# RWKV block of a two-part transformer: decay bias in the matrix product, other order of pieces, gate products moved to the end

## What is computed

```
r, k, v, w_lr, a_lr, g_lr = split(token_shift(p, mu))
log_decay = -softplus(-(w0 + tanh(w_lr) @ w2)) - 0.5
decay = exp(-exp(log_decay))           # = exp(-e^-0.5 * sigmoid(w0 + tanh(w_lr) @ w2))
a = sigmoid(a0 + a_lr @ a2)
g = sigmoid(g_lr) @ g2
kk = heads(k * k_k);  kk = kk / max(sqrt(sum(kk * kk)), 1e-12)
...                                     # recurrence over tokens, 8 heads of 64
y = group_norm(y) * ln_w + ln_b
y = (y + bonus) * g
merged = g_ret * (y_ret @ p_ret) + g_dsa * (y_dsa @ p_dsa) + g_rwkv * (y @ p_rwkv)
```

## Time and profile before

| what | value |
|---|---|
| median of 3 runs | 2798.94 us (2798.51 to 2799.71) |
| profiled execution | 2798.51 us, its span 2796.7 us |
| TensorE products / weight loads busy | 2599.5 us (93%) / 2008.1 us (72%) |
| VectorE / ScalarE busy | 1274.0 us (46%) / 836.0 us (30%) |
| mean granted TensorE clock | 0.987 |
| chain that ended last | TensorE 69%, DMA 20%, VectorE 6%, ScalarE 2% |

### The profile page before, as it was taken

How to read it: one execution, slowest core, us unless ns; L and a number is a source line. 1 busy time by engine, 2 the same in 40 slices (tenths; PEclk the granted TensorE clock), 3 DMA queues, 4 the chain that set the end, 5 groups by cost and what they waited for, 6 DMA issues and landing times.

```text
span 2796.7 us, 46123 instructions
## 1 busy us (share of the span) xinstructions
PE 2599.5 (93%) x19503; PEld 2008.1 (72%) x19503; DVE 1274.0 (46%) x1875; ACT 836.0 (30%) x1051; POOL 0.2 (0%) x4
## 2 busy tenths in 40 slices
PE   8899888879899888879999999999999999999998
PEld 8743433348543333369999899999899898899998
DVE  4610101037411000055566765655655658766555
ACT  4300000025210000033343442443433444523433
POOL 0000000000000000000000000000000000000000
PEclk9999999999999999999999999999999999999999
DMA  8689999973899999955563441455555544323553
GB/s 270 264 357 425 426 425 425 426 286 106 329 400 425 425 425 425 426 192 181 181 230 122 135 140 59 137 166 181 181 181 181 192 152 150 107 77 107 166 181 136
DMA packets 286519, 685.17 MB, mean 245 GB/s; under 512 B 11992, under 2 KB 217616, under 8 KB 236944
## 3 DMA queue, kind: packets, MB, share of 16 engines
q1 hardware_dynamic: 282792, 671.27, 63.6%
q10 hardware_dynamic: 3560, 11.45, 1.1%
HBM read 681.63 MB, written 1.05 MB: 244 GB/s over the span
## 4 chain that ended last, share of the span: by engine, by line
PE 69%; DMA 20%; DVE 6%; ACT 2%; issue 1%; DVEq 1%; SPq 0%; ACTq 0%; POOLq 0%
PE psum L419 68%; DMA weight_ring<-in_w_gate 14%; DMA weight_ring<-in_w_up 3%; DMA weight_ring<-in_w_down 2%; DVE weight_ring_parts L2066 1%; PE psum L427 1%; ACT weight_ring_parts L2058 1%; DVEq L552 1%; DMA weight_ring<-in_w_in_a 0%; DVE arena L3260 0%; SPq L1921 0%; DMA h_tok<-in_mem 0%; DMA weight_ring<-in_w_in 0%; DVE arena L1837 0%; DVE small L2778 0%
## 5 line engine op out<-in xcount | busy, mean ns | idle before, releaser
L419 PE MATMUL psum<-weight_ring_parts,arena_parts 128*128 128x256 f32 (+1 forms) x2992 | 666.4, 315 | 6.3 <-DVE arena_parts L2159 1.9
L2066 DVE TENSOR_TENSOR weight_ring_parts<-weight_ring,weight_ring_parts 128x2048 fp32r<-128x2048 f32 x217 | 496.5, 2290 | 338.0 <-ACT weight_ring_parts L2058 332.0
L419 PE MATMUL psum<-x_chan_parts,weight_ring_parts 128*128 128x256 f32 x3200 | 612.2, 282 | 12.9 <-DVE arena_parts L2155 7.7
L2058 ACT ACTIVATE weight_ring_parts<-weight_ring 128x2048 fp32r<-128x2048 f32 x217 | 414.9, 1913 | 465.7 <-POOLq L532 345.4
L419 PE MATMUL psum<-weight_ring,arena 128*64 128x512 f32 (+1 forms) x2112 | 474.8, 582 | 73.8 <-DMA weight_ring<-in_w_gate 39.1
L419 PEld LDWEIGHTS psum<-weight_ring_parts,arena_parts 128*128 128x128 f32 x2992 | 496.4, 189 | 42.9 <-issue 3.3
L419 PEld LDWEIGHTS psum<-x_chan_parts,weight_ring_parts 128*128 128x128 f32 x3200 | 509.0, 190 | 18.3 <-issue 12.9
L419 PE MATMUL psum<-arena 64*64 64x64 f32 (+7 forms) x4616 | 467.0, 335 | 29.3 <-DVE arena L1837 15.6
L419 PEld LDWEIGHTS psum<-weight_ring,arena 128*64 128x64 f32 (+1 forms) x2112 | 179.3, 140 | 361.4 <-issue 358.5
L419 PE MATMUL psum<-weight_ring_parts,x_chan_parts 128*128 128x256 f32 x2336 | 427.5, 285 | 2.3 <-DVE arena_parts L2155 2.2
L419 PE MATMUL psum<-arena_parts,weight_ring_parts 128*128 128x256 f32 x1536 | 419.0, 283 | 0.0
(11 more groups left out here) (324 smaller groups left out, 1713.6 us busy)
## 6 DMA issues: line engine op xcount, KB each, us to landing
weight_ring<-in_w_gate SPq DMA_DIRECT2D x92, 1024.0 KB, 23.2
weight_ring<-in_w_up SPq DMA_DIRECT2D x92, 1024.0 KB, 22.9
weight_ring<-in_w_in SPq DMA_DIRECT2D x70, 1024.0 KB, 5.0
arena<-in_w_down SPq DMA_DIRECT2D x64, 1024.0 KB, 22.5
weight_ring<-in_w_down SPq DMA_DIRECT2D x64, 1024.0 KB, 23.2
weight_ring<-in_ffa_w_in SPq DMA_DIRECT2D x44, 1024.0 KB, 7.1
weight_ring<-in_ffb_w_in SPq DMA_DIRECT2D x44, 1024.0 KB, 5.7
arena<-in_w_gate SPq DMA_DIRECT2D x36, 1024.0 KB, 18.5
```

What stands on the lines that cost most here:

```text
L419: return nc.tensor.matmul(*args, **kw)
L2058: nc.scalar.activation(HIGH[buf], ring[:, sl, :], ACT.Copy).then_inc(s_hi, 1)
L2066: nc.vector.tensor_tensor(ring_parts[:, sl, :], ring[:, sl, :], f32(HIGH[buf]), ALU.subtract).then_inc(s_split, 1)
```

## The change

The bias becomes one row, which TensorE adds to the decay piece with a product of a row of ones by the bias row. ScalarE reads the decay pieces from PSUM. The two decay pieces come first, then the two of the rates. The sums are written in four pieces again, but first two of inclusive sums and then two of exclusive ones, each for 256 channels; the exponentials follow suit. VectorE's low part of load 34 stands ahead of its reading of the head sums. The gate groups 2, 1, 1, 2 behind the solve are taken out and the last 12 become 18. In the tail the gate g multiplies the finished sum once, where it multiplied its two terms beforehand.

```diff
-        W0B = sb("decay_bias_rows", [P, 512])
+        W0R = sb("decay_bias_row", [1, 512])
...
-            s.e.dma_start(W0B[:, :], a["rwkv_w0_2"][l].partition_broadcast(P)).then_inc(s_load["w0"], 16)
+            s.e.dma_start(W0R[0:1, :], a["rwkv_w0_2"][bass.ds(l, 1), :]).then_inc(s_load["w0"], 16)
...
+            pe.e.wait_ge(s_load["w0"], pe.c["l_w0"].next())
...
-                pe.mm(ps[:, b, :], LR[0:64, 0, t * P:(t + 1) * P], LORA[0:64, :], start=True, stop=True).then_inc(s_full[b], 1)
+                pe.mm(ps[:, b, :], LR[0:64, 0, t * P:(t + 1) * P], LORA[0:64, :], start=True, stop=False)
+                pe.mm(ps[:, b, :], ones2[0:1, :], W0R[0:1, :], start=False, stop=True).then_inc(s_full[b], 1)
+            for c in range(0, 4, 2):
                 b = pe.take()
                 pe.e.wait_ge(s_free[b], pe.emptied())
                 for j in range(2):
-                    c = 2 * t + j
-                    last = pe.mm(ps[:, b, j * SEQ:(j + 1) * SEQ], LORA[64:128, c * P:(c + 1) * P],
+                    last = pe.mm(ps[:, b, j * SEQ:(j + 1) * SEQ], LORA[64:128, (c + j) * P:(c + j + 1) * P],
                                  LR[64:128, 0, :], start=True, stop=True)
                 last.then_inc(s_full[b], 1)
...
-            pe.e.wait_ge(s_a2p, pe.c["a2p"].next(T))
-            for c in range(4):
-                b = pe.take()
-                pe.e.wait_ge(s_free[b], pe.emptied())
-                for t in range(T):
-                    last = pe.mm(ps[:, b, t * 2 * P:(t + 1) * 2 * P], LWT[:, t, c * P:(c + 1) * P], cumulate,
-                                 start=True, stop=True)
-                last.then_inc(s_full[b], 1)
+            pe.e.wait_ge(s_free[(pe.pieces.n - 6) % BANKS], pe.read_out(pe.pieces.n - 6))
+
+            pe.e.wait_ge(s_free[(pe.pieces.n - 5) % BANKS], pe.read_out(pe.pieces.n - 5))
+            for m in (1, 0):
+                for c in range(0, 4, 2):
+                    b = pe.take()
+                    pe.e.wait_ge(s_free[b], pe.emptied())
+                    for j in range(2):
+                        for t in range(T):
+                            last = pe.mm(ps[:, b, j * SEQ + t * P:j * SEQ + (t + 1) * P],
+                                         LWT[:, t, (c + j) * P:(c + j + 1) * P], cumulate[:, m * P:(m + 1) * P],
+                                         start=True, stop=True)
+                    last.then_inc(s_full[b], 1)
...
-            gate_products(2)
             settled(4)
...
             for n in range(2):
-                gate_products(1)
...
-            gate_products(2)
             settled(4)
...
-            gate_products(12)
+            gate_products(18)
...
             for t in range(T):
-                s.skip()
-
-                s.e.wait_ge(s_v2a, s.c["v2a"].next(2 if t == 0 else 1))
-                nc.scalar.activation(LWT[:, t, :], LWT[:, t, :], ACT.Sigmoid).then_inc(s_a2p, 1)
+                b = s.take()
+                s.e.wait_ge(s_full[b], s.filled())
+                nc.scalar.activation(LWT[:, t, :], ps[:, b, :], ACT.Sigmoid).then_inc(s_free[b], 1)
...
-            nc.scalar.activation(RSS[:, :, :], RSS[:, :, :], ACT.Sqrt).then_inc(s_a2v, 1)
...
-            for c in range(4):
-                b = s.take()
-                s.e.wait_ge(s_full[b], s.filled())
-                sums = ps[:, b, :].rearrange("p (t m n) -> p m t n", t=T, m=2)
-                nc.scalar.activation(by_token_tile(PI, c), sums[:, 1], ACT.Exp, scale=-DECAY)
-                nc.scalar.activation(by_token_tile(IPI, c), sums[:, 1], ACT.Exp, scale=DECAY)
-                nc.scalar.activation(by_token_tile(PEX, c), sums[:, 0], ACT.Exp, scale=-DECAY).then_inc(s_free[b], 1)
+            s_root(RSS[:, :, :])
+            for c in range(0, 4, 2):
+                b = s.take()
+                s.e.wait_ge(s_full[b], s.filled())
+                nc.scalar.activation(flat(PI[:, c:c + 2, :]), ps[:, b, :], ACT.Exp, scale=-DECAY)
+                nc.scalar.activation(flat(IPI[:, c:c + 2, :]), ps[:, b, :], ACT.Exp, scale=DECAY).then_inc(s_free[b], 1)
+            for c in range(0, 4, 2):
+                b = s.take()
+                s.e.wait_ge(s_full[b], s.filled())
+                nc.scalar.activation(flat(PEX[:, c:c + 2, :]), ps[:, b, :], ACT.Exp, scale=-DECAY).then_inc(s_free[b], 1)
...
             v_merge_sparse(0)
+            v_ahead(34)
             v_rates_of_tokens(1.0, 1e-24, ALU.mult, ALU.max)
-            v.e.wait_ge(s_load["w0"], v.c["l_w0"].next())
-            rates = v.pieces.n + 1
-            for t in range(T):
-                b = v.take()
-                v.e.wait_ge(s_full[b], v.filled())
-                nc.vector.tensor_tensor(LWT[:, t, :], ps[:, b, :], W0B[:, :], ALU.add).then_inc(s_free[b], 1)
-                v.sync()
-                nc.vector.nop().then_inc(s_v2a, 1)
-                v.skip()
-            v_ahead(34)
-            v.skip(6)
+            rates = v.pieces.n + 2
+            v.skip(10)
             v_reciprocal_of_rates()
-
-            for n in (rates, rates + 2):
+            for n in (rates, rates + 1):
...
-            nc.vector.tensor_tensor(BON[:, :, :], BON[:, :, :], WG[:, :, :], ALU.mult)
-            v.sync()
-            nc.vector.tensor_tensor(YO[:, :, :], YO[:, :, :], WG[:, :, :], ALU.mult)
...
             v.sync()
+            nc.vector.tensor_tensor(YO[:, :, :], YO[:, :, :], BON[:, :, :], ALU.add)
+            v.sync()
             for c in (0, 2):
-                nc.vector.tensor_tensor(YO[:, c:c + 2, :], YO[:, c:c + 2, :], BON[:, c:c + 2, :], ALU.add).then_inc(s_v2a, 1)
+                nc.vector.tensor_tensor(YO[:, c:c + 2, :], YO[:, c:c + 2, :], WG[:, c:c + 2, :], ALU.mult).then_inc(s_v2a, 1)
```

More of the change, by code:

```diff
@@ L3091, in s_rwkv @@
                 for j in range(2):
-                    c = 2 * t + j
-                    last = nc.scalar.activation(WA[:, c, :], ps[:, b, j * SEQ:(j + 1) * SEQ], ACT.Sigmoid,
-                                                bias=pv("rwkv_a0")[:, c:c + 1])
+                    last = nc.scalar.activation(WA[:, c + j, :], ps[:, b, j * SEQ:(j + 1) * SEQ], ACT.Sigmoid,
+                                                bias=pv("rwkv_a0")[:, c + j:c + j + 1])
                 last.then_inc(s_free[b], 1)
@@ L3099, in s_rwkv @@
                 nc.scalar.activation(flat(WG[:, c:c + 2, :]), ps[:, b, :], ACT.Copy).then_inc(s_free[b], 1)
-            nc.scalar.activation(RSS[:, :, :], RSS[:, :, :], ACT.Sqrt).then_inc(s_a2v, 1)
-            def by_token_tile(x, c):
-                return x[:, c, :].rearrange("p (t n) -> p t n", t=T)
-            for c in range(4):
+            s_root(RSS[:, :, :])
+            for c in range(0, 4, 2):
                 b = s.take()
                 s.e.wait_ge(s_full[b], s.filled())
-                sums = ps[:, b, :].rearrange("p (t m n) -> p m t n", t=T, m=2)
-                nc.scalar.activation(by_token_tile(PI, c), sums[:, 1], ACT.Exp, scale=-DECAY)
-                nc.scalar.activation(by_token_tile(IPI, c), sums[:, 1], ACT.Exp, scale=DECAY)
-                nc.scalar.activation(by_token_tile(PEX, c), sums[:, 0], ACT.Exp, scale=-DECAY).then_inc(s_free[b], 1)
+                nc.scalar.activation(flat(PI[:, c:c + 2, :]), ps[:, b, :], ACT.Exp, scale=-DECAY)
+                nc.scalar.activation(flat(IPI[:, c:c + 2, :]), ps[:, b, :], ACT.Exp, scale=DECAY).then_inc(s_free[b], 1)
+            for c in range(0, 4, 2):
+                b = s.take()
+                s.e.wait_ge(s_full[b], s.filled())
+                nc.scalar.activation(flat(PEX[:, c:c + 2, :]), ps[:, b, :], ACT.Exp, scale=-DECAY).then_inc(s_free[b], 1)
             s.skip(2)
```

## The result

The changed kernel takes 2826.48 us, the median of 8 runs (2817.81 to 2839.44). The kernel before, run beside it, takes 2802.27 us (8 runs, 2798.51 to 2804.51). The ratio is 1.0083, 95% interval 1.0061 to 1.0105: about 24 us slower, where 6.5 us were forecast, and outside the range. Over all 33 executions of the changed kernel the times form two groups: 15 lie between 2814.8 and 2821.6 us, with a mean granted clock of 0.981 to 0.985, and 18 between 2824.4 and 2839.4 us, with 0.973 to 0.979. The kernel before has 0.987. The profiled execution (2830.59 us) is of the upper group.

A forecast was written before the change was run, and what follows sets the result against it. TensorE, busy for 93% of the span, was taken as the bound, with ScalarE pacing the decay stage. Decay 4.8 plus gate groups 1.7 gave 6.5 us on 2798.5, 2805.0, and 0.4 for the median: 2805.4 us, range 2801.5 to 2809.

The forecast's parts named there:

- The sign: Whole kernel: slower, 2805.4 us or +0.23%; chances slower 0.61, same 0.34, faster 0.05.
- TensorE's clock falls: Rival, decay stage: idle gaps lower the clock during WA1 to G1, up to 2.7 us a layer; chance 0.12.
- WA1 waits for the bank of the head sums: Decay stage: second rates piece waits for VectorE's late read of its PSUM bank; +2.5 and +2.1 us by layer.
- the row of four products: Decay stage: both decay pieces and both bias products at 0.90 us each, 3.6 us, finished before the bank is free.
- The total of this part: Decay stage, both layers: 2.5 + 2.1 + 0.2 = 4.8 us slower.
- My first rival: Decay stage: the late bank does not decide; 32 records in a row, 7.2 us; total 2800.8 to 2804.2; chance 0.24.
- One row costs what 64 or 128 cost: Decay stage: the one-row bias product taken at the 64-row product's full price, 0.90 us.
- Sums and exponentials, +0.1: Decay stage: new sums covered, reshaped exponentials end the head spreading 0.1 us later a layer.
- The bias row's load: ScalarE's queue behind the first FFN: 2 KB instead of 256 KB, effect nothing.
- Gate groups, +0.86 a layer: Solve and tail: six moved groups save 1.28 us and cost 2.14 at the end, 1.7 in all.
- The tail's extra pass, covered: Tail: VectorE's extra 1.3 us pass hidden behind 18 gate groups; without the moved groups it would cost 0.9.
- 0.2% as what can't be told: Whole kernel: a difference under 0.2% (5.6 us) is about what measurement can't tell from none.

The follow-up runs named there:

- e2: The changed kernel with the bias added by a product of 128 equal rows instead of one row; 2824.61 us, ratio 1.0068.
- e3: The changed kernel with the 128-row bias product and the gate groups back in their places behind the solve; 2818.53 us, ratio 1.0062.
- e1: The changed kernel with the gate groups 2, 1, 1, 2 back behind the solve and 12 at the end; 2819.43 us, ratio 1.0065.
- e7: The kernel before with only the one-row bias products added, VectorE copying where it added; 2814.52 us, ratio 1.0049.
- e12: The changed kernel with gate groups back and pieces in the order decay, bias, rates, decay, bias, rates; 2816.02 us, ratio 1.0057.
- e14: As e12, with VectorE reading the head sums ahead of the low part of load 34, as before; 2809.55 us, ratio 1.0031.
- e15: As e14, with the tail's two products by the gate back as in the kernel before; 2816.66 us, ratio 1.0061.
- e20: The kernel before with only the one-row bias products and the six gate groups moved to the end; 2819.81 us, ratio 1.0066.
- e5: The changed kernel with gate groups back and without the bias products (w0 left out); 2812.27 us, ratio 1.0048.
- e11: As e5, with the pieces in the order of before: decay, rates, decay, rates; 2815.55 us, ratio 1.0053.
- e17: The kernel before with only the low part of load 34 ahead of VectorE's read of the head sums; 2814.00 us, ratio 1.0048.
- c1: The kernel before, unchanged, run as a control under its own label; 2803.50 us, ratio 1.0005.
- e4: The kernel before with only the six gate groups moved to the end; 2803.24 us, ratio 1.0009.
- e4b: A repeat of e4 for another profile; 2804.36 us, ratio 1.0014.
- e13: As e11, with VectorE reading the head sums ahead of the low part of load 34, as before; 2809.15 us, ratio 1.0024.
- e16: The kernel before with only the new form of the sums and exponentials; 2801.51 us, ratio 1.0003.

## Why the prediction was wrong

The sign was right, the size was not. By its steps:

- **"TensorE's clock falls", chance 0.12, at most 2.7 us a layer: this is the step that failed.** It was priced as an idle between two bursts, for 2.71 us of products. What the runs show in its place is a fall while TensorE is busy, 13.7 and 10.2 us long, at 0.40 to 0.47 of its length: 6.5 us by e2 and e3 in layer 0, and 68.2 - 64.1 = 4.1 in layer 1. Count the decay stages of all profiled executions. With the bias products the clock falls in 14 of 18 passes (after, e1, e2, e3, e7, e12, e14, e15, e20, two layers each). Without them but with TensorE waiting 2.4 to 3.5 us for the head sums' bank it falls in 6 of 6 (e5, e11, e17). With neither it falls in 0 of 12 (before, c1, e4, e4b, e13, e16), though these have idles of up to 1.5 us. That the bias products and the late read each bring it down is shown.

What in the stretch with the bias products does it isn't: those with one and with 128 rows both do, and 4 of 18 passes escape. The traces narrow it down. In 10 of the 14 passes the fall comes 0.71 to 0.96 us behind the start of D0, and the first bias product begins only 1.09 to 1.34 us behind it; all ten last 13.7 us. D0 itself is already slowed there: 1.32 us for its records in layer 0 of after, 1.12 at 2.4 GHz. So in these passes it can't be the running of the bias product. What differs up to then is that D0 runs alone. In every kernel without the bias product a record of WA0 starts 0.01 us behind D0, as in this row of the kernel before, beside D0 at 1646.92 in the earlier trace rows:

```profile
1646.93 0.70 PE L419 MATMUL psum<-arena,norm_gain_bias 64*128 64x256 f32 x2
```

With the bias product WA0 starts 2.1 us behind D0 at the earliest. That D0 alone is what brings the clock down is argued, not shown: no run keeps WA0 from D0 without adding a product. That leaves the cause open, and with it how often the falls come; the medians of e14 and e13 lie together, those of e7 and the kernel before don't.

- **The fall seen as an idle gap.** The prediction weighed the rival by gaps alone. In e5, e11 and e17 the gap is there (2.4 to 3.5 us). Of the 14 falls with bias products 13 have none (in after, 14.00 us busy of 14, and 3.00 of 3 before them). The one in layer 1 of e12, which has the late read too, has a wait of 0.63 us for the head sums' bank ahead of it. The Trainium skill ("TensorE: Matmul & The Clock Gate", "Why this matters for your kernels") asks to avoid idle gaps between bursts; the first kind agrees with it, for the second the measurement decides.
- **The second fall, in the chunks.** 38.3 and 38.4 us with it (after, e2), 29.6 without (e4, e20): 8.7 us, with 20.5 us at 1.2 GHz. It came where two things met, a fall in the decay stage of the same layer and moved gate groups: in 2 of 4 such passes (layer 0 of after and of e2; not in layer 1 of after, nor in layer 0 of e20). With moved groups and no fall ahead of them it came in 0 of 6 passes, and with a fall and the groups in place in 0 of 16. Four passes are too few to call the link shown. It would explain part of the distance between the two groups of times, which is about 14 us; this is argued, not shown. The two groups of e2 fit it, e20 doesn't decide it. It stays open.
- **"WA1 waits for the bank of the head sums": the mechanism is right, its place in this kernel wrong.** The wait is there, 3.50, 3.21 and 3.31 us, once the bias products are gone. With them TensorE is its own bound. The term that was mis-sized is the row of four products, D0, D1 and the two bias products: 0.90 us each forecast, 1.05 measured. The sum had TensorE ready for WA1 4.5 us behind D0 (1651.4) and the bank free at 5.4 (1652.3). In layer 0 of e3, at full clock, the four take 4.2 us before WA0 begins, and the read of the head sums ends at 4.89, before WA1's turn. The table load then starts 8.78 us behind D0 where it was 6.29: +2.5 in layer 0, just as forecast, for another reason than the one given; that is luck. In layer 1 (e2) it is 8.78 against 5.60, +3.2 where 2.1 were forecast. The total of this part at full clock was 2.7 and 3.4 us for 2.6 and 2.2 forecast. Before, D and WA lie in different halves of the rows and run side by side, D0, WA0, D1 and WA1 together in about 2 us; the two bias products cost TensorE that overlap as well as their own length. My first rival (32 records in a row, 7.2 us) described it, with 7.97 us measured, and priced it at 0.8 us too little. The Trainium skill (the same page, "Packing small matmuls") says that products in different groups of rows run at once; the 12 records of D and WA side by side agree.
- **One row costs what 64 or 128 cost**: confirmed, 1.05 us for each (1.12 us for the pair of records).
- **Sums and exponentials, +0.1**: confirmed. e16 gives 0; e13 goes from D0 to the head spreading in 10.34 us against 10.20. The bias row's load: nothing, 424.7 against 424.8 to the Tanh.
- **Gate groups, +0.86 a layer**: 1.8 us saved instead of 1.28 (e4b). 2.1 are given back up to the next Square, as forecast (2.14), so +0.3 there; by the last Square of the program 2.4, so +0.6. The waits are those forecast.
- **The tail's extra pass, covered**: right. From the square of y to the next Square e4 and after both take 51.1 or 51.2 us, with the old tail and with the new one. Without the moved groups it costs 0.9 us, as forecast (e1: 50.0 against 49.1).
- **Chance between executions.** The prediction took 0.2% as what can't be told. The unchanged kernel's own 11 times span 9 us, its times beside all the runs 2797.44 to 2810.23, and kernels with falls that come and go span 20 and more (e20 20.3, e2 25.5). A range built from one trace has to allow for that. Also unexplained is some of e13: its stretches in the table account for about 2.0 us over the two layers, and its ratio is 1.0024, 6.7 us.

No version tried beats the kernel before; e16, which keeps only the new sums, equals it.

## What to carry to other kernels

When an edit puts products on the path in a stage where TensorE had short pieces overlapping, ask two questions ahead of the sum: does the added product share rows with its neighbour, so that it runs alone, and what would the stage cost at 1.2 GHz. If busy time grows and the work doesn't, read the granted clock in windows before looking for waits, and place the fall against the starts of the instructions: here it mostly came before the product under suspicion. Compare stretches between fixed instructions, and run the unchanged kernel as a control: here it moved 6.6 us by itself.

## What the runs showed of the hardware

- TensorE's clock fell from 2.4 to 1.2 GHz with TensorE busy all the time, in the middle of a stretch of fp32 products (4 products of 512 columns from 2456.51, the fall in the fourth), and stayed low for up to 13.7 us there, and for 20.5 us in the chunks, under continuous work. In ten passes it fell 0.71 to 0.96 us behind the start of D0.
- An idle doesn't decide it by its length alone. A wait of 2.39 us was followed by a fall in layer 1 of e17. At the mixer's start an idle of 2.52 us had one at its end in layer 0; in layer 1 one of 2.50, with two shorter ones of 0.35 and 1.39 behind it, left the clock at 2.4 GHz.
- It fell the same way with contraction over 1 and over 128 rows, and in 14 of 18 passes of nearly the same work. In e2, e3, e15 and e20 one layer has the fall and the other hasn't, with the same instructions, so it isn't fixed by the program alone.
- Two fp32 products on the same rows, one behind the other, took 1.05 us each for 512 columns. A product on the other half of the rows came beside them at little cost: 12 records of D and WA in 2.0 us (e13, 1652.65 to 1654.65).
- At 1.2 GHz a stretch that TensorE bounds loses 0.40 to 0.47 of the time it spends there: 6.5 us of 13.7, 4.1 of 10.2, 8.7 of 20.5.
